# Inverse roots of three recurrent heads by Newton steps on VectorE instead of ScalarE's root

## What is computed

```python
h_ml = mlstm_chunkwise(q_ml, k_ml, v_ml, gates_i, gates_f)      # (1, 512, 4, 128): num / max(|den|, exp(-m))
h_ml = rmsnorm(h_ml, ml_head_norm.reshape(ML_HEADS, ML_V))       # x * rsqrt(mean(x*x) + 1e-6) * g, per head
h_ml = h_ml * sigmoid(o_ml)
h_mla = causal_block_attention(q, k, kv[..., MLA_NOPE:])         # 8 latent heads
out = concatenate([h_ml, h_mla]) @ w_out
```

## Time and profile before

| | |
|---|---|
| median of 3 runs | 1511.37 us (1510.83 to 1511.81) |
| profiled execution, its own time | 1513.8 us |
| its span | 1512.0 us |
| mean granted TensorE clock | 0.998 |
| TensorE matmuls, busy | 1491.3 us (99%) |
| VectorE, busy | 1128.0 us (75%) |
| ScalarE, busy | 751.4 us (50%) |
| GpSimd, busy | 626.8 us (41%) |

### The profile page before, as it was taken

The page is one execution under the profiler, slowest core; times in us unless marked ns, Lnnn a source line. Parts: engine busy times, 40 slices in busy tenths (PEclk is TensorE's granted clock), DMA queues, the critical chain, the costliest instruction groups (busy, mean ns, idle before and its releaser), DMA issues.

```text
span 1512.0 us, 20174 instructions
## 1 busy us (share of the span) xinstructions
PE 1491.3 (99%) x6978; PEld 1231.2 (81%) x6978; DVE 1128.0 (75%) x1872; ACT 751.4 (50%) x1255; POOL 626.8 (41%) x280
## 2 busy tenths in 40 slices
PE   9999999999999999999999999999999999999998
PEld 7888888878888887888888888787778888888887
DVE  5689999997865445776776768788755887777776
ACT  6554333455562345754544345464963745444434
POOL 3455444332334432144444445451534344444451
PEclk9999999999999999999999999999999999999999
DMA  5343233345443323333333123233643432333551
GB/s 212 98 124 99 95 94 95 92 157 157 157 157 98 98 83 112 104 93 97 112 98 109 52 85 97 84 98 93 186 140 105 142 117 90 109 122 114 142 136 56
DMA packets 77026, 170.40 MB, mean 113 GB/s; under 512 B 22660, under 2 KB 39172, under 8 KB 76680
## 3 DMA queue, kind: packets, MB, share of 16 engines
q1 hardware_dynamic: 75920, 165.64, 35.2%
q10 hardware_dynamic: 1016, 3.61, 0.7%
HBM read 154.54 MB, written 14.69 MB: 112 GB/s over the span
## 4 chain that ended last, share of the span: by engine, by line
PE 87%; ACT 4%; DVE 4%; issue 3%; POOL 1%; DMA 1%; SPq 0%; DVEq 0%; ACTq 0%; POOLq 0%
PE bank L795 86%; DMA w_raw<-in_stream 1%; POOL w_lo L655 1%; ACT w_hi L1604 1%; DVE x_sq L2359 0%; ACT l_probs L2129 0%; DVE bias L2441 0%; ACT l_probs L2135 0%; ACT dn_first L1898 0%; POOL res L764 0%; DMA dn_raw<-in_stream 0%; PE bank L1214 0%; DVE res_tok L3421 0%; PE bank L905 0%; ACT ml_square L2080 0%
## 5 line engine op out<-in xcount | busy, mean ns | idle before, releaser
L655 POOL TENSOR_TENSOR w_lo<-w_raw,w_hi 128x1024 fp32r<-128x1024 f32 x191 | 473.2, 2487 | 518.1 <-ACT w_hi L1604 510.4
L795 PE MATMUL bank<-a_hi,w_hi 128*128 128x512 f32 (+1 forms) x1120 | 444.8, 397 | 2.2 <-DVE a_lo L3284 1.8
L795 PE MATMUL bank<-a_hi,w_lo 128*128 128x512 f32 (+1 forms) x1120 | 431.4, 385 | 0.0
L795 PE MATMUL bank<-a_lo,w_hi 128*128 128x512 f32 (+1 forms) x1120 | 431.2, 385 | 0.0
L1604 ACT CAST w_hi<-w_raw 128x1024 fp32r<-128x1024 f32 x199 | 204.6, 1046 | 174.9 <-DMA w_raw<-in_stream 174.5
L795 PEld LDWEIGHTS bank<-a_hi,w_hi 128*128 128x128 f32 x1120 | 210.5, 188 | 49.0 <-issue 4.2
L795 PEld LDWEIGHTS bank<-a_lo,w_hi 128*128 128x128 f32 x1120 | 210.6, 188 | 45.2 <-issue 3.4
L795 PEld LDWEIGHTS bank<-a_hi,w_lo 128*128 128x128 f32 x1120 | 210.4, 188 | 42.6
L667 POOL TENSOR_TENSOR dn_rest<-dn_raw,dn_second 128x1024 fp32r<-128x1024 f32 x39 | 93.7, 2431 | 248.3 <-DVE dn_rest L2734 248.3
L795 PE MATMUL bank<-dn_rest,f_hi 128*128 128x512 f32 x364 | 141.7, 389 | 0.0
L1898 ACT CAST dn_first<-dn_raw 128x1024 fp32r<-128x1024 f32 x54 | 55.6, 1047 | 157.9 <-DVE dn_raw L2715 157.9
(11 more groups left out here) (428 smaller groups left out, 2763.5 us busy)
## 6 DMA issues: line engine op xcount, KB each, us to landing
w_raw<-in_stream SPq DMA_DIRECT2D x199, 512.0 KB, 3.5
dn_raw<-in_stream SPq DMA_DIRECT2D x56, 512.0 KB, 3.6
p_parts<-d_parts SPq DMA_DIRECT2D x8, 640.0 KB, 3.9
d_turned<-p_parts SPq DMA_DIRECT2D x32, 160.0 KB, 3.3
l_turned<-p_parts SPq DMA_DIRECT2D x32, 160.0 KB, 3.1
p_parts<-l_parts SPq DMA_DIRECT2D x8, 384.0 KB, 3.3
res<-in_xT ACTq DMA_DIRECT2D x1, 2048.0 KB, 9.1
p_parts<-l_parts SPq DMA_DIRECT2D x8, 256.0 KB, 2.4
```

What stands on the lines that cost most here:

```text
L655: nc.gpsimd.tensor_tensor(w_lo[:, j, :], w_raw[:, j, :], w_hi[:, j, :].bitcast(F32), ALU.subtract).then_inc(w_lo_done, 1)
L795: return nc.tensor.matmul(o, l, r, start=start, stop=stop)
```

## The change

For the first three heads, ScalarE's root (L2085) and VectorE's reciprocal (L3124) go. In their place VectorE runs `inverse_root` in step 8, in front of the next head's diagonals: a first guess from the bits of the variance, taken as an integer, and three Newton steps of three operations each, ten chained operations on 128 by 4 numbers. The fourth head keeps the root and the reciprocal. ScalarE's squares of a head now also wait until the head before has its inverse roots.

```diff
+ROOT_SEED = float(0x5F3759DF)
+ROOT_STEPS = 3
...
                 if st == 7:
                     act.wait_ge(sems["ml_out"], 4 * (h + 1))
+                    if h >= 1:
+                        act.wait_ge(sems["ml_inv"], h)
                     for qb in range(TB):
                         m = A.activation(ml_square[:, qb * P:(qb + 1) * P], ml_block(qb, ML_V), ACT.Square,
                                          accum_out=mcol[:, 2, qb:qb + 1])
                     m.then_inc(sems["ml_sq"], 1)
-                if st == 8:
+                if st == 8 and h == ML_HEADS - 1:
                     act.wait_ge(sems["ml_var"], h + 1)
                     A.activation(mcol[:, 3, :], mcol[:, 2, :], ACT.Sqrt).then_inc(sems["ml_root"], 1)
...
+            def inverse_root(h):
+                part, x, y = mcol[:, 0, :], mcol[:, 2, :], mcol[:, 3, :]
+                dve.wait_ge(sems["ml_var"], h + 1)
+                chained(V.tensor_scalar(y.bitcast(I32), x.bitcast(I32), -0.5, ROOT_SEED, ALU.mult, ALU.add))
+                for i in range(ROOT_STEPS):
+                    chained(V.scalar_tensor_tensor(out=part, in0=y, scalar=-0.5, in1=y, op0=ALU.mult, op1=ALU.mult))
+                    chained(V.tensor_tensor(part, part, x, ALU.mult))
+                    m = V.scalar_tensor_tensor(out=y, in0=part, scalar=1.5, in1=y, op0=ALU.add, op1=ALU.mult)
+                    if i < ROOT_STEPS - 1:
+                        chained(m)
+                    else:
+                        m.then_inc(sems["ml_inv"], 1)
...
+                if st == 8 and h < ML_HEADS - 1:
+                    inverse_root(h)
                 if st == 9:
-                    dve.wait_ge(sems["ml_root"], h + 1)
-                    V.reciprocal(mcol[:, 3, :], mcol[:, 3, :]).then_inc(sems["ml_inv"], 1)
+                    if h == ML_HEADS - 1:
+                        dve.wait_ge(sems["ml_root"], 1)
+                        V.reciprocal(mcol[:, 3, :], mcol[:, 3, :]).then_inc(sems["ml_inv"], 1)
                     dve.wait_ge(sems["ml_inv"], h + 1)
```

## The result

The changed kernel takes 1516.94 us (median of 7 runs, 1516.58 to 1518.58), the kernel before, run beside it, 1511.81 (7 runs, 1510.81 to 1514.01). The ratio is 1.0032, with a 95% interval of 1.0022 to 1.0043: 4.8 us slower, 3.3 to 6.5. The profiled executions are 1517.25 us (span 1515.5) and 1513.8 (span 1512.0), 3.45 us apart.

What follows compares the result with a forecast made beforehand. TensorE, busy 99%, bounds the kernel, so only its waits at three handovers count: 0.9 + 0.7 + 0.7 = 2.3 us, plus 1.9 for GpSimd's hold, 4.2 us; 1515.6 us in the median, range 1511.8 to 1517.8.

Steps and rivals of the forecast that it cites:

- likeliest case: VectorE's steps plus GpSimd holding VectorE at the third handover: 3.0 to 5.4 us later, chance 0.47, own range 1514.4 to 1516.8.
- ten steps, first to diagonals: On VectorE in front of each head's diagonals, ten chained 128x4 steps move everything behind them by 1.9 us.
- first handover, TensorE: Head 0 to 1: VectorE's `hml` comes later and TensorE, already waiting for it, loses 0.9 us.
- second handover: VectorE's `sT` comes later; TensorE is 1.6 us late, 0.9 of which it had, so 0.7 more.
- third, by the queue and the hold together: Third handover: 0.7 us from VectorE's later queue plus 1.9 us from GpSimd's products holding VectorE's steps.
- sum at TensorE's third start: TensorE's delay over all three handovers: 2.3 us without the hold plus 1.9 for it, 4.2 us.
- Price of a step: VectorE's chained 128x4 steps start 0.20 us apart and last 0.16; ten make 1.9 us, bounds 1.2 and 4.7.
- The hold: Third handover: GpSimd's `res` products, shifted later, block VectorE's floor square and variance (L3107, L3110): 1.9 us, bounds 0 and 2.2.
- The queue's part: Third handover: 1.9 us of steps less VectorE's pauses and the 0.31 of slow L3107 gives 0.66, so 0.7 us.
- Clock: Rival: TensorE's clock also halves at the second handover, 1.6 us more, 5.8 in all, 1517.2 us; chance 0.15.
- Faster: Rival: ScalarE's loads end last and VectorE has room, so TensorE's waits and half clock go: 5.2 less, 1506.2; chance 0.08.
- Nothing happens: Rival: ScalarE's table loads stay where they were, so ScalarE wins nothing; no chance given.

Runs made afterwards that it cites:

- the two kernels with the products apart: GpSimd's last four of eight products moved behind its wait for the fourth head's diagonals: in the changed kernel 1514.21 us, in the kernel before 1511.89 us.
- the three kernels whose rows are shown: The changed kernel, 1516.94 us; the change with the first guess alone, 1510.41 us; the change with its ten steps behind the next head's diagonals, 1527.26 us.
- the same kernel with only the products moved: The kernel before with nothing but GpSimd's last four products moved behind the last head's diagonals: 1511.89 us, ratio 1.0001.
- four operations: The change with one Newton step in place of three, GpSimd's last four products moved behind its wait for the fourth head's diagonals: 1509.26 us, ratio 0.9983.

## Why the prediction was right

The sign and the cause were right, and the time came out 1.3 us above the 1515.6 forecast, inside the range and 0.1 us outside the likeliest case's own range (1514.4 to 1516.8). How near it came is in part luck, as the paragraph on the sum shows. Point by point, with 0.68 us taken off each start of the changed kernel:

| step of the prediction | forecast | measured |
|---|---|---|
| ten steps, first to diagonals | 1.9 | 1.82 |
| first handover, TensorE | +0.9 | +0.74 |
| second handover | +0.7 | +0.63 |
| third, by the queue and the hold together | +2.6 | +2.08 |
| sum at TensorE's third start | 4.2 | 3.45 |

*Price of a step.* Right: nine distances of 0.20 and a last 0.16, as the two chained steps of the earlier trace rows showed. The bounds of 1.2 and 4.7 were not needed. (What comes off ScalarE was put at 2.6 us a handover; two loads of 1.28 and the root's 0.20 make 2.8. It enters no sum.)

*First and second handover.* Right in place and size. ScalarE stands idle for 3.15 and 2.62 us, VectorE's pauses are used up, and TensorE waits for VectorE. By its own figures the second should have been 0.8: 1090.05 lies 1.69 us behind 1088.36, not 1.6. One thing the prediction did not name: at the first handover TensorE waits for `sT`, and at the second and third first for `ml_rows` (1.24 and 2.25 us), which is older work in VectorE's queue than `sT` there; the same queue delays all of them, so the sum did not suffer.

*Third handover.* The hold came where it was put. In the kernel before, the two steps took 0.71 us up to the transpose, the slow L3107 of 0.47 included; now they take 2.32 (1103.97 to 1106.29): 1.61 more, where 1.9 less the 0.31 of that slow row, 1.59, had been forecast. The queue's part was forecast at 0.97 before that 0.31 and came out at about 0.5. The term that was too large is this one: the pauses on the way to `sT` had been counted at 0.51 and 0.22, and VectorE had 0.2 more in front of a score mask (at 1103.93 in the kernel before), and 0.06 and 0.08 more in the two that had been counted. That the hold is a cause of its own, the two kernels with the products apart show: about 2 us for the hold that the change made, nothing for the move itself that can be told from no change. By the Trainium skill ("SBUF — State Buffer", "Who interferes with whom") VectorE's two-input instructions and GpSimd's reads exclude each other for a whole instruction; in the three kernels whose rows are shown the traces agree, with steps of 0.71 to 2.27 us that end 0.02 to 0.05 us behind an end of GpSimd's.

*Clock.* The rival did not come at the second handover: the matmul at 1091.15 takes 0.91 us, as before. At the third the half clock fell on other work. In the kernel before it slowed the latent scores' matmul at 1112.53 (1.72 us); that one takes 1.02 at 1116.64 now. In its place the recurrent scores at 1113.11 are slow (1.58 in place of 0.91), and that loss lies in the wait for `hml` of 0.78 us that TensorE had there before. So 0.7 us of the 3.45 came back, and 2.74 reached the matmuls at 1118.60, in agreement with the 2.8 behind the front in the spans. The prediction had the clock at the third handover as unchanged.

*The sum, and where luck came in.* TensorE's first matmul with `mix_hi` and `w_hi`, before and in the changed kernel:

```profile
1118.43 0.47 PE L795 MATMUL bank<-mix_hi,w_hi 128*128 128x512 f32 x1
```

```profile
1121.85 0.48 PE L797 MATMUL bank<-mix_hi,w_hi 128*128 128x512 f32 x1
```

From the floor step of the first handover to this matmul go 56.51 us before and 59.25 in the changed kernel; what comes behind it takes 393.3 to 393.7 us in all thirteen profiles. So the two traces differ by 2.7 us where the change acts, 1.5 less than the 4.2 forecast: 0.2 at the first two handovers, 0.5 in the queue's part of the third and 0.7 by the clock. Then the prediction went from the profile to the median by taking off 2.4 us, as in the kernel before; in the changed kernel the profile lies only 0.3 above its median (1517.25 and 1516.94). The two errors work against each other, and that the time came so near 1515.6 is luck to that extent.

The runs suggest why the 2.4 did not carry over. The profile of the kernel before has the half clock at the third handover; the same kernel with only the products moved has not (1.00 from 1110.99 to 1114.4), and takes 54.98 us for the stretch, 1.5 less. Of the 75 runs of the kernel before, 38 have a mean granted clock of 0.999 or 1.000 and a mean time of 1510.8 us, 37 have 0.997 or 0.998 and 1512.9; the changed kernel's seven all have 0.997 or 0.998. If the first 38 ran without the half clock at this place, the changed kernel loses 2.7 us against one half of the runs of the kernel before and 59.25 - 54.98 = 4.3 against the other half; the mean of both, 3.5, lies inside the measured 3.3 to 6.5. A run's mean does not say where the clock fell, so this is argued and not shown.

*Faster.* Its condition was nearer than the prediction put it. It gave the point from which it decides as 0.7 us of steps, from the first handover alone. With the products apart, four operations (0.8 us by their distance) still are 2.6 us faster than the kernel before, and ten (2.0 us) 2.7 slower, so that point lies between 0.8 and 2.0. Four operations make no handover worse: TensorE's waits are 0.23 us at the first, as before, 0.31 at the second in place of 1.31, and 0.60 and 0.78 at the third in place of 1.25 and 0.78. The room is VectorE's pause of 1.41 us at the second, which the prediction did not weigh in this rival. It changes no number of the forecast for ten steps, but for four it would have misled.

*Nothing happens* was excluded by the missing loads, as forecast.

What stays open: why nearly the same waits of TensorE are followed by the half clock in one profile and not in another (last section), and so how much of the 4.8 us is the clock.

## What to carry to other kernels

Moving work off an engine is worth only the waits that end on that engine, and what it costs on the other is read from that engine's pauses in its own order, at that place, not from its busy share: 2 us of small steps at each of three places, on a queue 75% busy, cost 4.8 us here, the relief of the other engine already counted. Small dependent steps belong where the engine stands idle anyway (GpSimd, in front of a wait of its own), with as few of them as the accuracy needs. And before small VectorE steps are put anywhere, look at what GpSimd does at that time: beside its work, each of them can cost a whole GpSimd instruction. A forecast that is carried from one profile to a median should ask whether that profile is a typical run.

## What the runs showed of the hardware

- A chain of VectorE steps beside GpSimd's work goes at GpSimd's pace: one step of 0.16 us at each end of a GpSimd instruction, so 1.18 to 2.27 us each. The first guess, a tensor_scalar with one input on 128x4 integers, was held like the others (1.65 us).
- A GpSimd operation on 128x4 numbers takes 0.19 to 0.20 us, and chained ones start 0.28 apart; some that run beside VectorE's diagonals or `mix_lo` take 0.32 to 0.62. Three of them in the kernel with three steps on GpSimd:

```profile
1065.14 0.20 POOL L750 TENSOR_TENSOR mcol<-mcol 128x4 f32<-128x4 f32 x1
1065.42 0.20 POOL L751 TENSOR_TENSOR mcol<-mcol 128x4 f32<-128x4 f32 x1
...
1084.03 0.62 POOL L752 TENSOR_SCALAR mcol<-mcol 128x4 f32<-128x4 f32 x1
```

- Waits of 1.25 and 0.78 us at the third handover of the kernel before were followed by half the clock (2.06 us for the values' matmul), waits of 1.24 and 0.78 in the same kernel with the products apart were not (1.13 us, granted clock 1.00). What decides it is not shown by these runs.
- The first 1,062 us, the same code in thirteen profiles, differ by 3.8 us from one to another. A comparison of two traces should therefore start from an event just ahead of the change.
